# Expert weights loaded matrix by matrix, in the order in which TensorE frees them, in a 32-expert layer stack

## The reference, cut to what matters

```
xs = t_pad[row_tok].reshape(n_blk, MOE_BLOCK, d)
def expert_block(args):
    xb, e = args
    a = jax.nn.silu(xb @ w1[e]) * (xb @ w3[e])
    return a @ w2[e]
yb = lax.map(expert_block, (xs, blk_exp)).reshape(cap, d)
y = jnp.zeros((n + 1, d), h.dtype).at[row_tok].add(yb * row_gate[:, None].astype(h.dtype))
```

## Time and profile before

| | us |
|---|---|
| median of 3 runs | 3587.39 |
| lowest and highest run | 3586.43, 3595.63 |
| the profiled execution | 3589.83 |
| its span (first to last instruction) | 3588.1 |
| TensorE busy | 3068.5 (86% of the span) |
| TensorE's granted clock, mean | 0.93 of full speed |
| expert stage, first weight issue to end of last down product | 618.8 to 1184.1 |

### The profile page before, as it was taken

The page is one execution under the profiler, slowest core; times in us unless marked ns, Lnnn a source line. Parts: engine busy times, 40 slices in busy tenths (PEclk is TensorE's granted clock), DMA queues, the critical chain, the costliest instruction groups (busy, mean ns, idle before and its releaser), DMA issues. The chain is left out here.

```text
span 3588.1 us, 34649 instructions
## 1 busy us (share of the span) xinstructions
PE 3068.5 (86%) x13906; PEld 1847.5 (51%) x13906; DVE 1046.3 (29%) x2162; ACT 747.3 (21%) x1627; POOL 164.6 (5%) x265
## 2 busy tenths in 40 slices
PE   7999974877787588999898999899949774888998
PEld 3448633444444465666455564455523343364674
DVE  3440622000000201055210273333126575200242
ACT  2111810000000102243210383100003110112341
POOL 0000001111110000000000020011100001000000
PEclk9999996899889799999999999999969887999999
DMA  6663432999999311110011200022233414011200
GB/s 228 234 229 124 177 147 62 347 351 365 361 364 358 115 48 32 42 48 24 0 36 60 83 2 1 24 94 87 88 101 132 150 63 148 0 41 53 77 1 24
DMA packets 244208, 441.15 MB, mean 123 GB/s; under 512 B 31420, under 2 KB 111820, under 8 KB 240725
## 3 DMA queue, kind: packets, MB, share of 16 engines
q1 hardware_dynamic: 234278, 416.81, 33.2%
q0 software_dynamic: 9776, 22.18, 1.8%
HBM read 408.73 MB, written 37.81 MB: 124 GB/s over the span
## 5 line engine op out<-in xcount | busy, mean ns | idle before, releaser
L2002 PE MATMUL moe_ph<-expert_weights,moe_x_T 128*64 128x256 f32 x2048 | 275.6, 429 | 100.4 <-issue 99.0
L344 PE MATMUL hyena_in_main<-hT,weight_slots 128*128 128x256 f32 (+1 forms) x1024 | 330.5, 486 | 1.4 <-PEq L985 1.4
L2002 PEld LDWEIGHTS moe_ph<-expert_weights,moe_x_T 128*64 128x64 f32 x2048 | 172.4, 155 | 206.7 <-issue 155.0
L344 PEld LDWEIGHTS hyena_in_main<-hT,weight_slots 128*128 128x128 f32 x1024 | 194.5, 190 | 137.2 <-issue 124.0
L344 PE MATMUL swa_in_main<-hT,weight_slots 128*128 128x512 f32 (+1 forms) x576 | 189.4, 489 | 6.6 <-DMA weight_slots<-b_w_in 5.2
L344 PE MATMUL mla_down_main<-hT,weight_slots 128*128 128x512 f32 (+1 forms) x448 | 168.4, 538 | 19.8 <-DMA weight_slots<-a_w_in 19.8
L1403 PE MATMUL qkv_main<-hT,weight_slots 128*128 128x512 f32 (+1 forms) x384 | 167.8, 580 | 0.9 <-PEq L985 0.9
L1194 PE MATMUL post_y<-expert_weights,hT 128*128 128x512 f32 x384 | 165.1, 592 | 0.0
L344 PEld LDWEIGHTS swa_in_main<-hT,weight_slots 128*128 128x128 f32 x576 | 109.9, 191 | 86.4 <-issue 73.7
L344 PE MATMUL mla_up_main<-expert_weights,weight_slots 128*128 128x512 f32 (+1 forms) x416 | 146.4, 511 | 2.8 <-PEq L985 2.4
L344 PEld LDWEIGHTS mla_down_main<-hT,weight_slots 128*128 128x128 f32 x448 | 88.0, 198 | 100.2 <-issue 75.0
(11 more groups left out here) (357 smaller groups left out, 4117.9 us busy)
## 6 DMA issues: line engine op xcount, KB each, us to landing
expert_weights<-w SPq DMA_DIRECT2D x96, 2048.0 KB, 15.2
first_w_out<-w_mod SPq DMA_DIRECT2D x12, 2048.0 KB
expert_weights<-w_mod SPq DMA_DIRECT2D x12, 2048.0 KB, 8.0
weight_slots<-w_in SPq DMA_DIRECT2D x16, 1024.0 KB
weight_slots<-c_w_in SPq DMA_DIRECT2D x16, 1024.0 KB
weight_slots<-a_w_in SPq DMA_DIRECT2D x14, 1024.0 KB
scr_spectra<-expert_weights SPq DMA_DIRECT2D x12, 1024.0 KB, 3.8
expert_weights<-scr_spectra SPq DMA_DIRECT2D x12, 1024.0 KB, 4.9
```

Of the source, the lines that this page charges most:

```text
L344: mm = pe.matmul(main[u][0:unit.rows, 0:unit.cols], lhsT, rhs, start=(c == 0), stop=(c == r.kc - 1))
L2002: mm = pe.matmul(bank[half * T:(half + 1) * T, 0:HF], x_T[:, c, :], w[:, c, half * HF:(half + 1) * HF], start=(c == 0), stop=(c == KD - 1))
```

## The change

`load_up` is cut in two: `load_gate` loads W1 and `load_up` loads W3. The semaphore `w13_in` of a slot is replaced by one for W1 and one for W3, so TensorE waits for W1 ahead of the first up product and for W3 ahead of the second. SP's loop now runs over the block b that TensorE works on and follows its order: behind the first up product of block b it loads W1 of expert b + 2, behind the second W3 of b + 2, and behind the down product of block b - 1 it loads W2 of expert b + 1. The two semaphores more make the pools of the stages one smaller each (67 numbers for 68).

```
@@ Stage
-    POOLS = ((99, 167), (167, 235))
+    POOLS = ((99, 166), (166, 233))
...
-        Stage.w13_in = [nc.alloc_semaphore(name=f"expert_w1_w3_in{k}", num=235 + k) for k in range(2)]
+        Stage.w1_in = [nc.alloc_semaphore(name=f"expert_w1_in{k}", num=233 + k) for k in range(2)]
+        Stage.w3_in = [nc.alloc_semaphore(name=f"expert_w3_in{k}", num=235 + k) for k in range(2)]
@@ ExpertWeights
+    def load_gate(self, sp, e):
+
+        sp.dma_start(self.W1[e % 2], self.w1[e]).then_inc(Stage.w1_in[e % 2], 16)
+
     def load_up(self, sp, e):
 
-        s = e % 2
-        sp.dma_start(self.W1[s], self.w1[e]).then_inc(Stage.w13_in[s], 16)
-        sp.dma_start(self.W3[s], self.w3[e]).then_inc(Stage.w13_in[s], 16)
+        sp.dma_start(self.W3[e % 2], self.w3[e]).then_inc(Stage.w3_in[e % 2], 16)
@@ experts_stage, SP
-                for b in range(experts.EARLY, E):
-
-                    sp.wait_ge(s_h3, b - 1)
-                    experts.load_up(sp, b)
-                    sp.wait_ge(s_py, b - 1)
-                    experts.load_down(sp, b)
+                for b in range(E):
+
+                    if b + 2 < E:
+                        sp.wait_ge(s_h1, b + 1)
+                        experts.load_gate(sp, b + 2)
+                        sp.wait_ge(s_h3, b + 1)
+                        experts.load_up(sp, b + 2)
+                    if experts.EARLY <= b + 1 < E:
+                        sp.wait_ge(s_py, b)
+                        experts.load_down(sp, b + 1)
@@ experts_stage, TensorE
-                    pe.wait_ge(Stage.w13_in[b % 2], (b // 2 + 1) * 32)
+                    pe.wait_ge(Stage.w1_in[b % 2], (b // 2 + 1) * 16)
                     pe.wait_ge(s_silu, b)
                     up_product(pe, ph1, x_T[b % 2], experts.W1[b % 2]).then_inc(s_h1, 1)
                     if b:
                         turn_act(b - 1)
+                    pe.wait_ge(Stage.w3_in[b % 2], (b // 2 + 1) * 16)
                     pe.wait_ge(s_act, b)
```

More of the change, by code:

```diff
@@ L1154, in _ @@
                     for e in range(experts.EARLY):
+                        experts.load_gate(sp, e)
                         experts.load_up(sp, e)
```

## The result

| | us |
|---|---|
| median after (4 runs, 3551.4 to 3561.2) | 3557.41 |
| median of the program before, in the same series | 3589.74 |
| ratio after to before, 95% interval | 0.9907 [0.9885, 0.9928] |
| the profiled execution after, its span | 3554.69, 3553.0 |

What follows compares the result with a forecast made beforehand. Expert-stage weight transfers were taken as the bound, their queue repeatedly running empty. From 3589.8 us, -33.3 (stream), -3.4 (start), -8 (end) and +3 (scatter) gave 3548.1, less 2.4 for the median 3546; range 3535 to 3568.

Steps and rivals of the forecast that it cites:

- The stream: Expert stage's weight transfers: without dips 197.6 MB at 381 GB/s take 518.7 us, 33.3 less than 552.
- The rival of the capped rate: Expert stage: memory gives 358 GB/s in the long run, leaving start and end only; 3579 us, chance 0.05.
- SP's order: Expert stage: W1 and W3 held behind the down product's wait empty the queue; ordering loads by release saves 33.3 us.
- The start: Start of the expert stage: first weight issue moves one up product earlier, gaining 3.4 us, bounds 0 and 3.5.
- The end: End of the expert stage: only one down product remains behind the last landing, gaining 8 us.
- if TensorE is late by the turning of the last rows it is 5: End of the expert stage: a late TensorE cuts the 8 us gain to 5.
- The scatter in the later loads: Behind the expert stage: the last scatter lands amid next stages' loads, costing 3 us, between 0 and 4.2.
- The sum of the stage: Expert stage with its start, end and last scatter: -33.3 - 3.4 - 8 + 3 = -41.7 us.
- new waits and semaphores: More semaphores and shorter pools add no long instruction; cost 0, at most 1 us, other stages keeping their length.
- less 2.4 for the median: Whole kernel: the profiled execution stood 2.4 us above the median of 3587.39, so 2.4 came off 3548.1.
- The rival of another loop: Expert stage: TensorE's block, slowed by a low clock, takes 17.7 us and bounds; 3565 us, chance 0.13.
- The case of the gather as the bound: Expert stage: gathers slowed by the full weight queue bound the block; 3602 us or more, chance 0.04.

Runs made afterwards that it cites:

- second series: The changed kernel run again with no edit, five rounds; 3552.0 us, ratio 0.9893 to the program before.
- two half programs: Changed kernel with W1 and W3 awaited together: 3556.62 us, 0.9899; program before with W1 and W3 loaded and awaited separately, old order: 3560.95 us, 0.9909.
- first trace: The profiled execution of the changed kernel in the series of the result, no further edit; 3554.69 us.
- The last program: Changed kernel with gathers one block earlier, the s_act wait dropped, and the next projection's two loads held behind the last scatter's landing; 3546.91 us, 0.9875.
- second trace of before: The program before run once more with no edit; 3586.09 us.
- early gathers: Changed kernel with each gather issued one block earlier: 3546.69 us, 0.9877; the same edit on the program before: 3592.61 us, 1.0002.

## Why the prediction was right, and where it was not

**The stream.** Right in size. 197.6 MB were to take 518.7 us at 381 GB/s; the second series of the changed kernel shows 518.2 us (617.0 to the landing at 1135.2) at 382. The long stretches of the earlier trace rows were the right rows, and not the mean of the earlier trace rows: 383 GB/s held for 502 us. The rival of the capped rate is out. "HBM Reference", Specifications (TRN2), of the Trainium skill gives 358 as a core's effective share, and says in the same section that a core streaming alone goes well above it, to about 425. My text took the first figure for a cap and left out the second; this core runs alone, and its 382 to 384 agree with the page that 358 is no cap here, while no run here reaches 425 over the stage.

**Why the dips went.** Half right. The prediction said that SP's order was the cause. The old order with separate waits loses its steady dips too (384 GB/s behind 750 us), and the new order with joint waits has only one left, 211 GB/s for 3 us. The dip needed both: three matrices issued together, and a whole block between the landing of the last of them and the next issue. My text said of the separate wait that in the middle it "only adds cover"; by itself it is worth 0.9909, most of the gain. What the text on record had right is that the two together leave no regular dip. What it did not ask is which of two sufficient cures does the work; only the two half programs show that either does.

**The start.** 9.05 us from the first up product to the first issue before, 6.14 after (first trace) and 5.6 (second): a gain of 2.9 and 3.5 us where 3.4 was said.

**The end.** 8 us forecast. In the second series the last down product ends 3.8 us behind the last landing in place of 11.7: 7.9 us. In the first trace it is 6.8 behind, a gain of 4.9 us: from the issue of the last W2 at 1129.53 TensorE has 15.4 us of its own work to the end of the last down product and waits for no transfer on the way, while the W2 lands after 8.6. TensorE was late there, not the matrix. That case stood in the working, though with another cause ("if TensorE is late by the turning of the last rows it is 5").

**The scatter in the later loads.** 3 us forecast. From the last scatter to the combine 13.7 us before, 16.3 in the second series (+2.6), 13.4 in the first trace. In the second series the scatter goes out 5.3 us behind the landing of the last W2 and lands in 5.2; in the first it goes out 8.3 us behind it, when by an estimate 3.2 of the 3.7 MB of loads are in (8.3 us at 383 GB/s), and lands in 2.6. The last program, which holds back 2 MB of these loads, shows by removal that they are the cause.

**The sum of the stage.** Up to the combine -42.6 and -39.55 in the traces; counted from the stage's own start, which came 0.7 and 1.5 us later for reasons outside the change, -43.3 and about -41. Forecast -41.7. Against the second trace of before they would be 1.9 us smaller, so the agreement is good to some 2 us, not better.

**The step that failed** is the last of the sum: new waits and semaphores "0, at most 1 us", with all other stages keeping their length. At the output of the window attention 1.5 to 3.2 us are lost (between 2050 and 2285) in every changed program but the last. That is some 3 of the 3.3 to 8.4 us that are missing by the ratios: forecast 1.16% (41.7 of 3589.8), measured 0.93 and 1.07%. An experiment that added 32 waits that are always met, and nothing else, produced the same 3 us in the trace of the program before. The first trace after lost another 3 us or so in steps too small to name, which the second did not. A second term is at fault for the forecast of the time itself: "less 2.4 for the median". The median of the program before in the series of the result is 3589.74 and not 3587.39, so these 2.4 us should not have been taken off; with them the forecast would have been 3548.

**The rival of another loop.** By its own sign it has come: TensorE waits for `moe_x` at 29 blocks, the clock stays at 0.90, one product of three is slow. By its price it has not: it was to make a block 17.7 us, and TensorE's block is 16.93. My text named that wait as a sign that the forecast is wrong. It is not one, since a wait that ends before the stream needs the room costs nothing. But the room is thin: I had put it at 1.6 us (15.7 against 17.3), and with the down product slow it is 0.3 (16.93 against 17.23), as the dip at 1123 to 1131 shows. That the loop stayed under the stream was luck in part: with one slow product a block the text itself put it at 17.7, above the stream, and nothing in the working says why it should come to less. The case of the gather as the bound was priced by a landing of 9.7 us or more. The gather issued at 1115.95, amid the stream, let the turning start at 1122.21, 6.3 us later; over the stage the gathers land in 6.7 us in the median and 7.8 at most.

Two readings of rows in the prediction are off and enter no sum: the first bytes come 1.2 us after an issue by its own two numbers (618.81 and 620), not some 2, and the slices of the stage are not flat at 357 to 365 but 347 and 351, then 358 to 365.

## What to carry to other kernels

A stream that stands still at intervals has a cycle: from an issue to the landing that releases the consumer, through what the consumer does, to the next issue. Count the bytes in the queue against the part of the cycle behind the landing; either more bytes in the queue (issue in the order of release) or a shorter path (wait for each matrix apart) cures it, and the second cure adds little to the first. After it, the wait that the profile shows on the compute engine says what that engine stands for, not what bounds the stage: the byte rate does. Take the pace of a stream from its landings and not from its issues, which follow the engine that frees the rooms; an experiment that shrinks the transfer shows how close the next loop is.

## What the runs showed of the hardware

- The stream ran at 382 to 384 GB/s in the mean over 500 us on a lone core, and at 381 with half of W2 left out and TensorE at full clock (1.00); a DMA share of 1.04 to 1.05 went with it each time.
- A short wait in a block can be followed by a lower granted clock, and the sum of the waits does not tell by how much. With 65.7 us of gather waits in 29 pieces (2.3 us in the mean) the clock is 0.90 over the stage, and the down product behind the wait takes some 5.3 us and not 3.65. With early gathers TensorE waits longer in all, 93.6 us in 75 pieces (1.2 us in the mean), and the clock is 0.98. Its levels are 2.4 GHz (full) and 1.2 GHz: over the down product at 1107.81 the mean is 0.69, with 0.50, the lower level, from 1108 to 1111 and 1.00 at its end; the 3.65 us are those of the full level.
- A 4 KB load took 3.1 to 3.6 us to be used when an instruction load of q8 began behind its issue (10 traces), and 1.6 to 1.7 us when that load lay ahead of it (4). Why 32 waits more move it, and 32 fewer do not move it back, stays open; no run here controls where it falls.
- Removing a wait made nothing faster and the clock lower (the early gathers in the program before), since it lengthened another wait.
